# A streaming encoder step on one core: indexer queries for selecting tokens only, a merged sample tile, and reordered hand-overs around memory attention

## What is computed

```
q, k, v, iq, ik, iw, zu, zv = split(rms_norm(x, g_mix_pre) @ w_in)
score = sum_h iw[h] * relu(iq[h] . ik * 64**-0.5)   # 8 indexer heads of 64
a = softmax attention over the 256 best admissible keys (prompt), 80 (sample)
s = gmlp_mix(layer_norm(gelu(zv)))                  # chunked spatial gate
x = x + rms_norm(concat(a, gelu(zu) * s) @ w_o, g_mix_post)
x = x + rms_norm(mem_attend(rms_norm(x, g_mem_pre)) @ w_mo, g_mem_post)
x = x + rms_norm(relu(rms_norm(x, g_ffn_pre) @ w1)**2 @ w2, g_ffn_post)
```

## Time and profile before

| | |
|---|---|
| median of 3 runs | 1674.92 us (1671.49 to 1677.46) |
| the profiled execution's own time | 1671.01 us |
| its span | 1669.3 us |
| mean granted clock of TensorE | 0.983 of 2.4 GHz |
| busy PE, DVE, ACT, POOL | 1582.0, 899.9, 622.2, 472.7 us |
| moved by DMA | 108.29 MB, 65 GB/s on average |

### The profile page before, as it was taken

The page is one execution under the profiler, slowest core; times in us unless marked ns, Lnnn a source line. Parts: engine busy times, 40 slices in busy tenths (PEclk is TensorE's granted clock), DMA queues, the critical chain, the costliest instruction groups (busy, mean ns, idle before and its releaser), DMA issues. The chain is left out here.

```text
span 1669.3 us, 23326 instructions
## 1 busy us (share of the span) xinstructions
PE 1582.0 (95%) x8523; PEld 1376.8 (82%) x8523; DVE 899.9 (54%) x1522; ACT 622.2 (37%) x1288; POOL 472.7 (28%) x328
## 2 busy tenths in 40 slices
PE   5989999999799989998999999999999999999997
PEld 5976899978566668787878899998888999888886
DVE  6328899999555655314574433334444333434436
ACT  6247576973666743224543212112121221111121
POOL 5233112128766333112024122212111221212132
PEclk9999999999899989998999999999999999999999
DMA  6222311121200043233042111111101111110106
GB/s 208 60 70 64 89 39 51 45 70 48 59 30 30 14 139 115 81 108 102 23 148 76 51 51 50 41 47 38 51 25 50 50 50 38 49 39 31 44 26 195
DMA packets 88199, 108.29 MB, mean 65 GB/s; under 512 B 6080, under 2 KB 65216, under 8 KB 88128
## 3 DMA queue, kind: packets, MB, share of 16 engines
q1 hardware_dynamic: 88128, 107.35, 20.8%
HBM read 88.05 MB, written 19.28 MB: 64 GB/s over the span
## 5 line engine op out<-in xcount | busy, mean ns | idle before, releaser
L155 POOL TENSOR_TENSOR w_lo_ring<-w_raw_ring,w_hi_ring 128x1024 fp32r<-128x1024 f32 (+1 forms) x97 | 234.1, 2424 | 786.9 <-ACT w_hi_ring L149 786.4
L2143 DVE TENSOR_TENSOR f_y<-f_y,ps 128x512 f32<-128x512 f32 x252 | 173.0, 687 | 210.7 <-PE ps L2228 210.7
L186 PE MATMUL ps<-hth,w_hi_ring 128*128 128x384 f32 (+2 forms) x1176 | 267.4, 331 | 4.3 <-PEq L1802 1.8
L186 PE MATMUL ps<-htl,w_hi_ring 128*128 128x384 f32 (+2 forms) x1176 | 266.1, 330 | 0.0
L186 PE MATMUL ps<-hth,w_lo_ring 128*128 128x384 f32 (+2 forms) x1176 | 266.0, 330 | 0.0
L2228 PE MATMUL ps<-w_hi_ring,f_fh 128*128 128x512 f32 x576 | 226.0, 396 | 4.3 <-DVE f_y L2143 2.7
L2228 PE MATMUL ps<-w_lo_ring,f_fh 128*128 128x512 f32 (+1 forms) x576 | 219.8, 391 | 0.0
L186 PEld LDWEIGHTS ps<-hth,w_hi_ring 128*128 128x128 f32 (+1 forms) x1176 | 202.7, 188 | 7.5 <-issue 5.3
L186 PEld LDWEIGHTS ps<-hth,w_lo_ring 128*128 128x128 f32 (+1 forms) x1176 | 202.5, 188 | 0.6
L186 PEld LDWEIGHTS ps<-htl,w_hi_ring 128*128 128x128 f32 (+1 forms) x1176 | 202.3, 188 | 0.6
L2228 PE MATMUL ps<-w_hi_ring,f_fl 128*128 128x512 f32 x512 | 199.8, 390 | 0.0
(11 more groups left out here) (248 smaller groups left out, 2574.2 us busy)
## 6 DMA issues: line engine op xcount, KB each, us to landing
w_raw_ring<-in_w SPq DMA_DIRECT2D x64, 512.0 KB, 3.8
w_raw_ring<-in_w_in SPq DMA_DIRECT2D x24, 512.0 KB, 3.8
n_xin<-in_x_prompt SPq DMA_DIRECT2D x8, 512.0 KB, 5.8
w_raw_ring<-in_w_o SPq DMA_DIRECT2D x8, 512.0 KB, 3.9
oe_x<-in_x_prompt SPq DMA_DIRECT2D x8, 512.0 KB, 4.6
x<-oe_new SPq DMA_DIRECT2D x8, 512.0 KB, 5.2
me_x<-x SPq DMA_DIRECT2D x8, 512.0 KB, 4.1
x<-me_new SPq DMA_DIRECT2D x8, 512.0 KB, 5.0
```

The source lines that it names most:

```text
L155: pool.tensor_tensor(self.lo[:, slot, 0:width], self.raw[:, g % 2, 0:width], self.hi[:, slot, 0:width].bitcast(F32), ALU.subtract).then_in ...
L186: last = pe.matmul(c.ps[0:width, bank + b, 0:size], part[:, slot, k * width:(k + 1) * width], x[:, k, o:o + size], start=(k == 0 and n == ...
L2143: dve.tensor_tensor(out, out, ps[:, u % 2, :], ALU.add).then_inc(y_added, 1)
```

## The change

1. Indexer queries are made for tokens 256 to 1087 alone, in two blocks of 416 columns. The first two query tiles are made in `norm_inputs`, in pieces from token tile 6 on; `index_scores` makes the other two.
2. `mix_output` splits the first four groups of tiles 0 and 1 first, and multiplies these halves before the last four rows of `w_o`. The sample is taken before the last prompt tile; its high and low parts stand side by side as 128 rows, so that two matmuls replace three, and ACT and DVE add the two halves.
3. Both hand-overs make two blocks of the next stage's first two weight tiles (`next_product`) before, between and after the last transposes.
4. `memory_attend` loads keys, two `w_mo` tiles, then values; transposes keys before query tiles 1 and 2; starts with the first head pair of two token tiles under query tile 3; and lets POOL split `w1` tiles only after the last unit's output.
5. Two semaphores of the epilogue become one, and its scratch tile moves in memory.

```diff
+QB_FROM = P * (min(256, SEQ // 4) // P)
+QB_SIZE = (T - QB_FROM) // 2
+QB = [(QB_FROM, QB_SIZE), (QB_FROM + QB_SIZE, QB_SIZE)]
...
 def IQ_BANK(j):
-    return 4 if j % 2 == 0 else 1
+    return (4, 6, 0, 2)[j]
+def iq_piece(c, pe, j, b, n):
+    return gemm_features(c, pe, j, IQ_BANK(j), blocks=(b, ), ks=(range(0, 3), range(3, 6), range(6, KD))[n], tb=QB)
...
-    FIRST_AT = 3
+    PIECES = {6: [(0, 0, 0), (0, 0, 1)], 7: [(0, 0, 2), (1, 0, 0)], 8: [(1, 0, 1), (1, 0, 2)],
+              9: [(0, 1, 0), (0, 1, 1)], 10: [(0, 1, 2), (1, 1, 0), (1, 1, 1), (1, 1, 2)]}
+    READY = [-(-(o + size) // P) for o, size in QB]
...
+                for j, b, n in PIECES.get(t, ()):
+                    if b == 0 and n == 0:
+                        c.w.wait(pe, j)
+                    pe.wait_ge(lo_done, READY[b])
+                    last = iq_piece(c, pe, j, b, n)
...
-            for j in range(1, 4):
+            for j in (2, 3):
                 c.w.wait(pe, j)
-                if j >= 2:
-                    pe.wait_ge(iq_lo, 4 * (j - 1))
-                gemm_features(c, pe, j, IQ_BANK(j)).then_inc(c.w.used, 1)
+                gemm_features(c, pe, j, IQ_BANK(j), tb=QB).then_inc(c.w.used, 1)
...
+def next_product(c, pe, e, w, n, j, b):
+    w.wait(pe, n + j)
+    if j == 0 and b == 0:
         pe.wait_ge(e.normed, NT - 1)
+    pe.wait_ge(e.lo_done, 3 * (b + 1) if j == 0 else NT - 2 + b)
+    gemm_features(c, pe, j, 2 + 3 * j, w=w, blocks=(b, ))
...
+def end_bank(t):
+    return 4 + 2 * (t % 2) if t < NT - 1 else 0
+AHEAD_OF = {NT: [(0, 0), (0, 1)], NT + 1: [(1, 0)]}
...
+    ORDER = list(range(NP - 1)) + [NP, NP - 1]
...
+            high(FIRST, 0)
+            high(FIRST, 1)
+            for n in range(REST):
+                c.w.split_hi(act, n, n)
+                if n < 2:
+                    high(SECOND, n)
+                else:
+                    high(ALL, ORDER[n])
+            for p in range(REST, NT):
+                high(ALL, ORDER[p])
...
+                if t == S_AT:
+                    act.wait_ge(e.stored[t % 2], 16 * (t // 2))
+                    act.wait_ge(e.xn_done, t - 1)
+                    act.activation(side, ps[DEC:P, 2 * (t % 2):2 * (t % 2) + 2, :], ACT.Copy).then_inc(side_done, 1)
...
+                            both, high = (out, xs[:, k, :], wh[k][:, n]), (out[0:DEC, :], xs[:, k, 0:DEC], wl[k][:, n])
+                            mms = [both, high] if k < KD - 1 else [high, both]
...
+            pe.wait_ge(cat_lo, 1)
+            products(0, range(NG))
+            pe.wait_ge(cat_lo, 2)
+            products(1, range(NG))
+            for k in range(NG, KD):
+                c.w.wait(pe, k - NG)
...
+                last = products(0, (k, ))
...
+            for p in range(2, NT + 2):
+                if p < NT:
+                    pe.wait_ge(cat_lo, p + 3)
+                    pe.wait_ge(e.normed, p - 1)
+                    products(p, range(KD)).then_inc(y_done, 1)
+                for j, b in AHEAD_OF.get(p, ()):
+                    next_product(c, pe, e, ahead, REST, j, b)
+                e.transposes(pe, p - 2)
+            next_product(c, pe, e, ahead, REST, 1, 1)
...
+    DONE = {0: (2, ), 1: (2, )}
+    units = [(0, 0), (1, 0), (0, 1), (1, 1)] + [(t, hp) for t in range(2, NT) for hp in range(2)]
+    KEYS_BY = {1: 0, 2: 1}
...
-                sync.dma_start(vm[:, s], v[0, 0].rearrange("(b p) h d -> p b (h d)", p=P)).then_inc(kv_in, 16)
-            for n in range(AHEAD, 8):
+            for n in range(AHEAD, 6):
+                c.w.load(sync, n, tiles[n])
+            for s, (k, v) in enumerate(((c.o_mkp, c.o_mvp), (c.cache_mem_k, c.cache_mem_v))):
+                sync.dma_start(vm[:, s], v[0, 0].rearrange("(b p) h d -> p b (h d)", p=P)).then_inc(v_in, 16)
+            for n in range(6, 8):
                 c.w.load(sync, n, tiles[n])
             for n in range(AHEAD):
                 c.w.load(sync, 8 + n, by_features(c.w1[0])[n])
...
+            pool.wait_ge(pv_done, len(units))
             for n in range(2):
                 c.w.split_both(pool, 8 + n, n)
...
+            for j in range(3):
+                if j in KEYS_BY:
+                    keys(KEYS_BY[j])
+                queries(j)
+            pe.wait_ge(q_done, 4)
+            pe.wait_ge(k_done, 2)
+            logits(0)
+            logits(1)
+            queries(3, range(0, 5))
+            pe.wait_ge(q_done, 6)
+            transposes(0)
+            transposes(1)
+            queries(3, range(5, KD))
+            outputs(0)
             pe.wait_ge(q_done, 8)
+            for u in range(2, len(units) + 3):
...
-                    gemm_features(c, pe, j, 2 + 3 * j, blocks=range(3) if s or j else (2, )).then_inc(a_done, 1)
+                    gemm_features(c, pe, j, 2 + 3 * j, blocks=range(3) if s else (2, )).then_inc(a_done, 1)
```

More of the change, by code:

```diff
@@ L354, in _ @@
                 tr.then_inc(tr_done, 1)
[L356 to L363, removed]
+                for j, b, n in PIECES.get(t, ()):
[3 more added lines that the diff above has]
+                    last = iq_piece(c, pe, j, b, n)
+                    if b == 1 and n == 2:
+                        last.then_inc(c.w.used, 1)
 def index_scores(c, m):
@@ L1899, in _ @@
+            maxima(0)
+            maxima(1)
+            scales(0)
+            scales(1)
+            for u in range(2, len(units) + 4):
+                if u < len(units):
+                    maxima(u)
+                if 2 <= u - 1 < len(units):
+                    scales(u - 1)
+                if u >= 4:
+                    lows(u - 4)
             for t in range(NT + 2):
@@ new lines, in queries, with logits @@
+            def queries(j, ks=range(KD)):
+                if ks[0] == 0:
+                    w.wait(pe, j)
+                    if j >= 2:
+                        pe.wait_ge(q_done, 2 * (j - 1))
+                last = gemm_features(c, pe, j, 2 + 3 * (j % 2), w=w, blocks=DONE.get(j, range(3)), ks=ks)
+                if ks[-1] == KD - 1:
+                    last.then_inc(w.used, 1)
+            def logits(u):
+                t, hp = units[u]
+                r, s = rows_of(t), int(t == NP)
+                if u >= 2:
+                    pe.wait_ge(exp_done, 2 * (u - 1))
+                for x in range(2):
+                    last = pe.matmul(ps[0:r, u % 2, x * NMEM:(x + 1) * NMEM], qm[:, 2 * hp + x, tok(t)], km[:, s, 2 * hp + x, :], start=True, stop=True)
+                last.then_inc(lg_done, 1)
@@ new lines, in transposes, with outputs @@
+            def transposes(v):
+                r = rows_of(units[v][0])
+                pe.wait_ge(scaled, 2 * v + 2)
+                if v >= 2:
+                    pe.wait_ge(pt_done, v - 1)
+                for x in range(2):
+                    for b in range(MB_):
+                        o = (2 * x + b) * P
+                        last = pe.transpose(ps[:, 2 + v % 2, o:o + r], pr[0:r, v % 3, x, b * P:(b + 1) * P], c.ident[0:r, 0:r])
+                last.then_inc(tr_done, 1)
+            def outputs(v):
+                t, hp = units[v]
+                r, s = rows_of(t), int(t == NP)
+                if v == 0:
+                    pe.wait_ge(v_in, 32)
+                pe.wait_ge(pt_done, v + 1)
+                if v >= 2:
+                    pe.wait_ge(o_lo, v - 1)
+                for x in range(2):
+                    h = 2 * hp + x
+                    for b in range(MB_):
+                        last = pe.matmul(ps[:, 4 + v % 2, x * P:x * P + r], vm[:, s, b, h * P:(h + 1) * P], pt[:, v % 2, 2 * x + b, 0:r],
+                                         start=(b == 0), stop=(b == MB_ - 1))
+                last.then_inc(pv_done, 1)
@@ L1954, in _ @@
+                    logits(u)
+                if 2 <= u - 2 < len(units):
+                    transposes(u - 2)
+                if 1 <= u - 3 < len(units):
+                    outputs(u - 3)
             for n in range(4, 8):
```

306 lines of the change are left out of this document (145 added, 161 removed).

## The result

The changed kernel takes 1651.58 us in the median of 4 runs (1649.43 to 1653.68), the kernel before, run beside it, 1673.2 us (1669.42 to 1677.46): a ratio of 0.987 with a 95% interval of [0.9849, 0.9892]. The prediction was 1650.9 us, -24.0; measured are -21.6 here and -23.6 where the changed kernel was run again (1652.22 against 1675.77). The profiled execution after has a span of 1647.7 us for 1669.3, at a mean granted clock of 0.989 for 0.983.

The account below looks back on a forecast made before the run. TensorE, busy 95% of the span, was taken as the bound. Terms -11.0 - 4.8 - 3.6 - 2.1 - 6.2 + 2.1 - 2.4 + 4.0 sum to -24.0, from median 1674.92 to 1650.9 us; range 1641 to 1663.

Parts of the forecast that it names:

- Queries: Indexer queries: two blocks of 416 columns for three, products from token tile 6; -11.0 us, bounds -8 to -14.
- about 10 matmuls at half speed +2.0: First indexer-query products: about 10 matmuls at half speed add 2.0 us, within the queries' forecast.
- The rival in which the clock stays low: Normalisation: short PE bursts leave 1.2 GHz through the query matmuls; 1684.8 us, chance 0.03.
- its absorption: Selection on DVE sets the end, so the queries' 11.0 us lead is lost; 1661.9 us, chance 0.05.
- Mixing: Mixing output's start: third tile starts at 622.35 for 627.15, after a 3.2 us wait; -4.8 us, bounds -2 to -8.
- sample tile: Mixing output's sample tile: two matmuls for three, 16 of 48 gone; -3.6 us.
- first hand-over: From mixing output to memory queries: waits covered, a new 1.8 us key wait; -2.1 us, bounds 0 to -4.
- Units under the last query tile: Memory attention: early logits start the pipeline under the last query tile; -6.2 us, bounds -3 to -8.
- Weight splits later: Memory output: late POOL splits delay the gains, third tile waits 2.4 us; +2.1 us, bounds 0 to +5.
- Second hand-over: Before w1's third tile: barrier 4.6 us later, 3.0 us wait for POOL's clearing and split; -2.4 us, bounds +1 to -5.
- Clock: Behind five new waits: lower clock costs between 0 and 8.0 us, half taken; +4.0 us.
- first rival: New waits take the hand-overs' place, with SP, POOL and DVE orders costing their upper bounds; 1660.1 us, chance 0.20.

Follow-up runs that it names:

- both experiments on the queries: Indexer-query part alone on the kernel before: 1660.86 us, 0.9921; that part taken back in the changed kernel: 1661.54 us, 0.9932.
- the square moved first: Changed kernel with the mixing epilogue's first square ahead of ScalarE's wait for all input splits: 1648.17 us, one run.
- the keys apart: Changed kernel with a separate semaphore for each of the two key loads: 1651.93 us, one run.
- The square: Changed kernel with early units and late splits each kept or undone; key transposes to output product: both 77.1 us, splits early 79.4, units behind 78.2, neither 82.1.

## Why the prediction was right, and where it was not

**Queries.** The gain was 13.1 us, for 11.0. 96 matmuls take 18.1 us, 0.188 each, as worked out. The difference is the start: "about 10 matmuls at half speed +2.0" did not come in this execution, and the first piece started at 31.47, not 32.1. That is the execution's luck and not a mis-sized term: in seven of eleven profiles 5 to 11 matmuls do run at half speed, and the transposes at 73.0 to 74.4 lie around the forecast of 74.0. The rival in which the clock stays low would have needed 155 of them. The lead reached the end whole; its absorption is refuted by both experiments on the queries.

**Mixing, sample tile, first hand-over.** -4.4, -3.4 and -1.8 for -4.8, -3.6 and -2.1, with the waits at the places named. The chain that was given for the third tile (last split, square, POOL, multiply) is shown by the square moved first, the key wait by the keys apart.

**Units under the last query tile** is the step that failed in its mechanism, though its size looks right (-5.6 for -6.2). The hold by POOL's last split that it reckoned with came (1.44 us for 0.17), but the wait behind it had stood one pair earlier before the change. The step gave the whole gain to the early start. The square shows that the early units by themselves bring 1.1 to 2.7 us and the late splits 2.3 to 3.9 in this stretch, together 5.0 of the 5.6 (82.1 - 77.1). The row that proves it was in the prediction, the 2.50 us of two scalings beside a split; it says that the later splits free these steps, but no term of the sum holds that. The Trainium skill, SBUF — State Buffer, section SBUF: two separate sides, says that whichever of GpSimd and DVE, in some of its operations, starts first holds the pair of ports that they share for a whole instruction; the trace agrees, 0.62 us free and 2.51 beside a split that began ahead. Clock is in these amounts: 5.1 us are lost in this stretch before, 3.4 with both parts undone, 1.7 in the changed kernel's two profiles. So 1.7 us came back with these two parts, and 1.7 with neither; with what, the runs leave open.

**Weight splits later** was sized too low, +3.8 for +2.1. The gains were used just when forecast: 832.2 less the 25.5 us of lead is 806.7, the multiply's row. PE came earlier: it had two tiles ready 1.6 us sooner than in the rows before, since those held a clock loss (818 to 831 us at 0.87, 1.7 us). Taken over both stages, "units" and "splits later" were forecast to bring 4.1 us together, and undoing both changes nothing: 99.1 us for 99.5.

**Second hand-over.** The 3.0 us for clearing and split came to 2.98. But the barrier moved by more than forecast. PE at the start of the last three transposes and behind the barrier, before (its second row is in the earlier trace rows) and after:

```profile
878.01 1.07 PE L1633 MATMUL ps<-ident,me_xn 128*128 128x128 f32 x8 [0.45 <-DVE htl L1642]
```
```profile
856.22 1.03 PE L1649 MATMUL ps<-ident,me_xn 128*128 128x128 f32 x8
...
876.11 0.38 PE L190 MATMUL ps<-hth,w_hi_ring 128*128 128x320 f32 x1 [0.45 <-PEq L1887]
```

That is 19.9 us for 14.3 (892.35 - 878.01), 5.5 more and not 4.6, so -1.3 for -2.4.

**Clock.** The term of +4.0, half of 0 to 8.0, met three losses of 1.7 us, 5.1, in one execution and five, 8.5, in the next, one of these at mixing's start, where the old kernel has one too. That the waits cause those behind them is shown by the profiles in which they are gone. Behind the gains' wait (3.9 to 4.4 us) a loss of 1.7 us stands in all seven profiles that have the wait, and in none of the four without it. Behind the clearing's (3.0 us) it stands in all nine, and in neither of the two where the wait is 1.3 us or less. Behind the one before the third mixing tile (2.6 us) it stands in six of eight, and in none of the three where the wait is 1.0 us or less. So whether a wait draws one is not settled by its length alone. Nor does a loss need such a wait: the kernel before loses 1.7 us at the start of the output product behind 0.78 us. The term left out the other side: the kernel before lost 13.7 us between attention and the first down product in both its profiles, so on balance 5.2 to 8.6 us of clock came back. The stage terms hold that unsaid, since they set products at full speed against today's starts.

So the sum, inside its range of 1641 to 1663, came out 2.4 us off by errors that partly cancel, and so its closeness is in part luck: the queries gave 2.1 more in this execution; the gains took 1.7 more and the second hand-over 1.1 more; 2.7 us belong to the short execution before; and the clock term was counted on top of stages that hold most of their losses already. Of the first rival's bounds that of the gains was neared (+3.8 of +5), and in the second execution that of the clock (6.8 behind four of the five waits, of +8).

## What to carry to other kernels

A load that waits in a queue behind a semaphore makes everything behind it late: before delaying work on one engine, look at what stands behind its consumers on SP's queue, and issue small loads with no dependence first. In this kernel a wait of 2.5 to 4 us on a full PE cost its length and, in most executions, 1.7 us of clock behind it. A difference of two single profiles moves by as much, so a stage is to be read in several executions, and the price of a part is to be taken from a square of both changes, on and off, where two parts touch the same stretch. A clearing or a copy with a late user does not belong at the head of an engine's queue behind a barrier.

## What was not expected of the hardware

The clock losses come in equal portions: 1.68, 1.73 and 1.69 us for three waits of different length, 2.45, 4.03 and 2.98 us (length times one minus the granted clock in the windows above). Two executions of the changed kernel, with spans of 1647.7 and 1650.3 us, differ by two of them between attention and the first down product, 5.1 against 8.5. And the releaser in a bracket can be an innocent one: where PE waited for two semaphores, the profile named ScalarE's relu, and moving the split's order took the wait from 1.30 to 0.30 us.
